# Another order of the side work around the first attention stage of a fused transformer kernel

## The reference

```python
cond = silu(c)                                   # one row of 1024
mod = cond @ ada_w[i] + ada_b[i]                 # 6 * 1024 values: shifts, scales, gates
h = rms_norm(x, norm_mix[i]) * (1.0 + sc1) + sh1
q, k, v = split(h @ w_in, 3)                     # 16 heads of 64
q = rms_norm(q, q_gain) * 64 ** -0.5;  k = rms_norm(k, k_gain)
p = softmax(q @ k.T + bias)                      # band of chunks, relative bias
x = x + g1 * ((p @ v) @ w_out)
h = rms_norm(x, norm_ffn[i]) * (1.0 + sc2) + sh2
x = x + g2 * (square(relu(h @ w1)) @ w2)
```

## Time and profile before

| | |
|---|---|
| time, median of 3 runs (lowest to highest) | 1117.07 us (1115.54 to 1119.04) |
| time of the profiled execution | 1119.04 us |
| its span in the trace | 1117.4 us |
| mean granted TensorE clock | 0.957 of full speed |
| busy: PE, DVE, ACT, POOL | 96%, 69%, 50%, 8% of the span |
| the chain that ended last | 80% on PE |

### The profile page before, as it was taken

One profiled execution on the slowest core, in us unless ns is written; L12 is line 12 of the kernel. 1 busy time (PEld: TensorE's weight loads), 2 busy tenths in 40 slices (PEclk: granted clock), 3 DMA queues, 4 the chain that ended last, 5 costly groups with the idle time before them and its releaser, 6 DMA issues.

```text
span 1117.4 us, 18346 instructions
## 1 busy us (share of the span) xinstructions
PE 1073.6 (96%) x6096; PEld 923.0 (83%) x6096; DVE 766.9 (69%) x1352; ACT 554.4 (50%) x933; POOL 94.1 (8%) x146
## 2 busy tenths in 40 slices
PE   6999999999999999999999999999999989799897
PEld 6887776999899788889998789998878768688775
DVE  5798766988876667777877554565487564686573
ACT  1556775354434457444443443454365572556562
POOL 0121101000000100100000000000011020120100
PEclk9799997999999899999999899999999989899999
DMA  9866654778786458765765365456166410457211
GB/s 369 322 242 222 213 191 170 267 279 281 269 297 241 165 191 292 254 231 206 260 224 180 99 214 195 151 190 215 47 220 225 131 57 20 136 200 215 79 33 52
DMA packets 58071, 219.12 MB, mean 196 GB/s; under 512 B 6532, under 2 KB 12420, under 8 KB 51880
## 3 DMA queue, kind: packets, MB, share of 16 engines
q1 hardware_dynamic: 49232, 170.02, 44.5%
q0 software_dynamic: 5760, 41.95, 10.4%
q10 hardware_dynamic: 3032, 6.57, 1.8%
HBM read 217.46 MB, written 1.06 MB: 196 GB/s over the span
## 4 chain that ended last, share of the span: by engine, by line
PE 80%; issue 8%; DVE 4%; DMA 3%; ACT 3%; POOL 1%; DVEq 0%; ACTq 0%; SPq 0%; POOLq 0%
PE ps L1596 24%; PE ps L1597 23%; PE ps L1598 23%; PE ps L1691 2%; DMA ada_raw<-in_adastream 2%; PE ps L1663 2%; PE ps L1681 1%; PE ps L1645 1%; ACT ada_raw L631 1%; DVE w_lo L949 1%; PE ps L1655 1%; POOL rinv L440 1%; PE ps L1958 1%; PE ps L2064 1%; DMA arena<-in_adastream 1%
## 5 line engine op out<-in xcount | busy, mean ns | idle before, releaser
L949 DVE TENSOR_TENSOR w_lo<-raw,w_hi 128x1024 fp32r<-128x1024 f32 (+1 forms) x318 | 358.8, 1171 | 62.0 <-ACT w_hi L534 56.0
L534 ACT ACTIVATE w_hi<-raw 128x1024 fp32r<-128x1024 f32 (+1 forms) x318 | 308.4, 1008 | 129.8 <-DMA raw<-in_wstream 94.2
L1596 PE MATMUL ps<-h_hi,w_hi 128*128 128x256 f32 x704 | 202.3, 287 | 0.5 <-DVE h_lo L1030 0.3
L1597 PE MATMUL ps<-h_lo,w_hi 128*128 128x256 f32 x704 | 200.7, 285 | 0.0
L1598 PE MATMUL ps<-h_hi,w_lo 128*128 128x256 f32 x704 | 200.7, 285 | 0.0
L1596 PE MATMUL ps<-w_hi,h_hi 128*128 128x512 f32 (+1 forms) x480 | 192.7, 401 | 3.2 <-DVE h_lo L1030 3.2
L1597 PE MATMUL ps<-w_lo,h_hi 128*128 128x512 f32 (+1 forms) x480 | 187.3, 390 | 0.0
L1598 PE MATMUL ps<-w_hi,h_lo 128*128 128x512 f32 (+1 forms) x480 | 187.0, 390 | 0.0
L1596 PEld LDWEIGHTS ps<-h_hi,w_hi 128*128 128x128 f32 x704 | 136.6, 194 | 3.5 <-issue 2.0
L1596 PE MATMUL ps<-w_hi,a_hi 128*128 128x512 f32 x352 | 137.4, 390 | 0.7 <-DVE a_lo L1359 0.7
L1597 PEld LDWEIGHTS ps<-h_lo,w_hi 128*128 128x128 f32 x704 | 136.7, 194 | 0.7
(11 more groups left out here) (186 smaller groups left out, 1341.9 us busy)
## 6 DMA issues: line engine op xcount, KB each, us to landing
raw<-in_wstream SPq DMA_DIRECT2D x296, 512.0 KB, 5.3
ada_raw<-in_adastream POOLq DMA_DIRECT2D x40, 1024.0 KB, 5.1
ada_raw<-in_adastream SPq DMA_DIRECT2D x4, 1024.0 KB, 9.2
arena<-in_adastream SPq DMA_DIRECT2D x4, 1024.0 KB, 10.7
raw<-in_wsmall SPq DMA_DIRECT2D x22, 128.0 KB, 2.2
row<-in_gate_rows ACTq DMA_DIRECT2D x5, 512.0 KB, 4.3
row<-in_params ACTq DMA_DIRECT2D x2, 769.0 KB, 4.1
x<-in_x SPq DMA_DIRECT2D x1, 1024.0 KB, 9.4
```

The costliest lines, as they stand in the source:

```text
L534: act.activation(w_hi[:, c % SPLIT, at], raw[:, n, 0:width // 2], ACT.Copy)\
L949: nc.vector.tensor_tensor(w_lo[:, c % SPLIT, at], raw[:, (2 * c + h) % RAW, 0:width // 2], w_hi[:, c % SPLIT, at].bitcast(F32), ALU.subtract)\
L1596: nc.tensor.matmul(dst, sh, mh, start=start, stop=False)
L1597: nc.tensor.matmul(dst, sh, ml, start=False, stop=False)
```

## The change

Nothing is added or taken away. On ScalarE `split(8)` moves ahead of the two value copies and the units 4 and 5. On VectorE the two masks move from ahead of `ada_part(9)` to behind `split(8)`, and `split(8)` moves ahead of the units 4 and 5. In the tables, piece 11 is scaled one head later (2 and 3) and summed at head 4 in place of 3; piece 13 is scaled at heads 8 and 9 in place of 5 and 8, and summed at 9 in place of 8; piece 15 is scaled at 10 and 11 in place of 11 and 12, and still summed at 12; piece 16 is summed at heads 12 and 13 in place of 13 and 14. The orders of TensorE, GpSimd and SyncE are the same instruction for instruction.

```diff
-SCALED_ADA = {1: (11, 0), 2: (11, 1), 5: (13, 0), 8: (13, 1), 11: (15, 0), 12: (15, 1),
-              14: (17, 0), 15: (17, 1), 16: (18, 0), 17: (18, 1)}
+SCALED_ADA = {2: 11, 8: 13, 10: 15, 14: 17, 16: 18}
@@ ScalarE @@
             unit_hi(0)
             unit_hi(1)
+            split(8)
             value_copy(2, 0)
             value_copy(2, 1)
             unit_hi(4)
             unit_hi(5)
-            split(8)
@@
-                if h in SCALED_ADA:
-                    a, q = SCALED_ADA[h]
-                    scaled(a, range(4 * q, 4 * q + 4))
+                if h - h % 2 in SCALED_ADA:
+                    scaled(SCALED_ADA[h - h % 2], range(4 * (h % 2), 4 * (h % 2) + 4))
@@ VectorE @@
             q_heads(1)
+            ada_part(9, 9)
+            unit_lo(0)
+            unit_lo(1)
+            split(8)
             dve.wait_ge(s_bias, 32)
             mask(row[:, 0:D])
             mask(gate[:])
-            ada_part(9, 9)
-            unit_lo(0)
-            unit_lo(1)
             unit_lo(4)
             unit_lo(5)
-            split(8)
@@
-                if h in (3, 8, 12, 16):
-                    scaled_sum({3: 11, 8: 13, 12: 15, 16: 17}[h])
-                if h in (0, 1, 4, 5, 10, 11, 13, 14):
-                    a, q = {0: (10, 0), 1: (10, 1), 4: (12, 0), 5: (12, 1), 10: (14, 0),
-                            11: (14, 1), 13: (16, 0), 14: (16, 1)}[h]
+                if h in (4, 9, 12, 16):
+                    scaled_sum({4: 11, 9: 13, 12: 15, 16: 17}[h])
+                if h in (0, 1, 4, 5, 10, 11, 12, 13):
+                    a, q = {0: 10, 4: 12, 10: 14, 12: 16}[h - h % 2], h % 2
```

## The result

The changed kernel took 1135.03 us, the median of four executions (1127.31 to 1136.43); the kernel before, run beside it, took 1118.05 (1115.54 to 1125.39, four as well). The ratio is 1.012, with a 95% interval of 1.008 to 1.017: slower, as forecast, but by more. 1135.0 lies above the range of 1120.0 to 1130.5. Three of the four executions of the kernel before are those that the forecast started from. The profiled execution took 1133.17 us, with a span of 1131.5.

What follows compares the result with a forecast made beforehand. PE, busy 96% of the span, was taken as the bound, so only its waits and clock could matter. Waits and the lost old stretch gave +5.8, new slow stretches +3.4: +9.2 on 1117.07, 1126.3 us; 8-in-10 range 1120 to 1130.5.

Steps and rivals of the forecast that it cites:

- The gain at head 8's product: Heads 8 to 9: with piece 13's sum behind head 9's maximum, PE's 1.31 us wait falls to about 0.1, -1.2.
- Place 1: First head: PE's scores wait for unit 4's subtraction, now behind chunk 8's halves and the masks; +2.2 us.
- place 2: Head 6: piece 11's later sum delays the normalised queries, so PE's transposes wait 3.3 us, not 0.87; +2.4 more.
- the old slow stretch: PE's half-speed clock from 140 to 143.5 us, behind the 1.31 us wait, goes with that wait; -1.7 us.
- head 9's product: Product with head 9's values: PE waits for a copy queued behind piece 15's first half, which awaits its load; +5.7 us.
- behind it: After head 9's product: piece 17's load comes in time, so most of PE's 1.85 us waiting at 157 to 163 goes; -1.4.
- A: Rival: the same waits but no new slow clock stretch; +5.8 us, 1122.9; chance 0.15.
- B: Rival: the waits hide in one another, the 5.7 us shrinking to 2.6 or less; about 1118.5 us; chance 0.10.
- C: Rival: no slower, even a little faster, because the first head's order is no bound; 1114.7 us; chance 0.05.
- D: Rival: more than three slow stretches, or longer ones after the 5.7 us stop; +12 to +14, about 1130; chance 0.10.
- The clock's term: Three longer PE waits may each bring a half-speed stretch of 1.7 us; two taken, +3.4, bounds nothing to 5.1.
- How the numbers follow: Final step setting chances (forecast 0.60) and ranges: one to three stretches plus a microsecond of scatter, 1123.5 to 1129.

Runs made afterwards that it cites:

- e7: The kernel before with only piece 13's sum moved from head 8 to head 9; 1119.23 us, ratio 0.9981 (0.9948 to 1.0014).
- e1: The changed kernel with the old order before the first head restored, new tables kept; 1128.70 us, ratio 1.0056 to the kernel before.
- e2: The changed kernel with the old tables restored, new order before the first head kept; 1126.67 us, ratio 1.0025 to the kernel before.
- b0_again: The kernel before run again with no edit; 1122.62 us, ratio 0.9996 to the kernel before beside it.
- e3: The changed kernel with one-row filler products in TensorE's waits at head 6 (12) and for head 9's copy (22); 1130.89 us, 2.5 below the changed kernel.
- e6: The kernel before with 7 one-row filler products in TensorE's 1.31 us wait; 1124.64 us, ratio 1.002 to the kernel before.

## Why the forecast was wrong

**Direction, mechanism and waits: right.** In the first trace all four waits came at their places with their releasers, within 0.2 us: 2.23 for 2.2, 3.18 for 3.3, 5.52 for 5.7, 0.68 for 0.86. In the second the third was 3.57, behind a slow stretch that the first did not have. The gain at head 8's product came too; e7 has it alone in its trace, though its time is not clear of no change. The stage took 10.1 us more in the first trace of the changed kernel and 10.5 in the second, against +9.2.

**The terms of the sum, from the first trace.** Place 1 was 2.25 for 2.2, place 2 2.33 for 2.4. VectorE began unit 4 at 79.74 us where 80.85 was worked out, but the whole trace ran 1.10 us ahead there. At head 8's product 1.60 us came back for 1.4, the old slow stretch gave 1.59 for 1.7, head 9's product cost 5.69 for 5.7, and behind it 1.92 came back for 1.4. The waits so give +5.2 for +5.8. The new slow stretches cost 1.6 and 3.4, 5.0 us for 3.4. That the stage's total lies within a microsecond of the forecast is in part luck: the two errors have opposite signs.

**The rivals.** A (no slow stretch) fell: in both traces slow stretches followed the wait at head 6 and the one for head 9's copy. B (the waits hide) fell with the trace itself: head 9's product waited 5.52 us, not 2.6 or less, and e1 and e2 add up within their errors. C (no slower) fell with the waits for `k_lo`. D, longer or more slow stretches at about 1130, came nearest in the mechanism as in the time.

**The clock's term was mis-sized.** "I take two, 3.4": there were two in the first trace, but the second, from 148.2 to 158.5 us, was no short one, and together they cost 5.0. The medians say the same by subtraction: 10.8 less the 5.8 forecast for the waits is 5.0 (6.0 with the other fillers), with an error of a microsecond or more. What the prediction quoted beside it from the Trainium skill ("TensorE: Matmul & The Clock Gate", Part 1), that the number of slow products differs between runs of one kernel, was the right reading: b0_again had no slow stretch behind a wait of 1.31 us, before had one.

**The step that failed is "How the numbers follow".** Its base, 1117.07 us, was taken as the kernel's time, and the range gave "a microsecond for the runs' scatter". The kernel's median is 1122.6 us, and single executions scatter by 4.2 us. The miss of 8.7 us splits, to a tenth, into 5.5 for the base (1122.6 - 1117.1), 1.6 for the change itself, the clock above all (10.8 - 9.2), and 1.7 for the four executions of the changed kernel (1135.0 - 1133.35). Even with the change's price known exactly the forecast would have been 1117.1 + 10.8 = 1127.9, 7 us under the measured time. The scatter could have been suspected from the trace: its slow stretches lose some 48 us (1117.4 x (1 - 0.957)), 1.7 us of it in the stage, and three short ones more or less make up nearly all of the forecast's own range of 1123.5 to 1129. The sentence that 3.4 us can be told from no change was wrong in the same way: a median of three carries an error of about 3 us on either side of a comparison.

## What to carry to other kernels

Where a producer, a sum, the reload of its slot and the next use form one chain (here 2.4 + 0.3 + 5.0 us), moving the sum later moves the reload, and a use moved earlier then stops whatever is queued behind it. Read a trace's slow stretches as a scatter of the time, and take no three executions for the kernel's median while they make up several per cent. Fill waits, if at all, with products of the full height: one row of zeros kept the engine busy in the profile, but behind 4.92 us of it (e3) and 1.68 us (e6) the clock fell.

## What the runs showed of the hardware

Fillers of 1x512 for 4.9 us were followed by a clock of 0.57, fillers of 128x512 of ones for 4.9 us by 1.00; at head 6, 2.8 us of the former were followed by 1.00 too. Whether the rows or the values matter was not tried apart. All 86 fillers in the latter shape took 12 us off the kernel before (1122.6 to 1110.5).

The clock's record can be missing. The first stretch of the changed kernel shows 93 products in 22 us at 0.53,

```profile
21.00:43.00 22.00, 22.00 (x93) 18.79 (x93) 17.54 (x40) 7.76 (x12) 1.32 (x2) 0.53 1.00 391
```

and that of e1 as many a microsecond, at 1.00:

```profile
23.00:43.00 20.00, 20.00 (x85) 17.47 (x86) 13.72 (x34) 5.40 (x10) 1.33 (x2) 1.00 1.00 390
```

The products' own lengths settle it. Those of 512 columns in e1's trace start 0.43 us apart and last 0.63 up to 47.5 us, and then start 0.23 apart and last 0.39, with the same clock of 1.00 on record:

```profile
44.11 0.63 PE L1593 MATMUL ps<-w_hi,h_hi 128*128 128x512 f32 x1
...
47.88 0.39 PE L1593 MATMUL ps<-w_hi,h_hi 128*128 128x512 f32 x1
```

So a mean clock may be compared between traces only where this stretch is read alike (0.947 and 0.962 in these two).
